# Sixteen of the prompt's expert rows moved from the merge into the latent q and k part of a diffusion trunk step

## The chip, the cores and the metric

The kernel runs on one core of a Trainium2 chip. The metric is the device time of one execution in microseconds (us). A core has TensorE (PE, matrix products), VectorE (DVE), ScalarE (ACT), GpSimd (POOL) and SyncE (SP), which each work through a program of their own in order and wait for one another on semaphores. SP issues the loads of the weights. POOL issues the gathers of expert rows, and each gather costs POOL an instruction before the DMA engines move anything.

## What is computed

The reference is a trunk of two layers over 128 prompt tokens and 512 latent tokens, all in float32. In each layer, and with the same weights for both kinds of tokens:

- an adaptive norm gives `h`; from it four branches are made: pooling over 2 to 16 neighbours, neighbourhood attention, a gated convolution over 31 tokens (`u = a * sigmoid(b)`, a depthwise convolution, a layer norm, SiLU), and differential attention; q and k are normed per head, and in the latent's differential branch they are rotated by position;
- the branches are merged with sigmoid gates and projected, `x = x + g1 * y`;
- a second norm, then the expert layer: each token takes 8 x 16 of 16384 experts and computes `sum(gate * gelu(u[e] . h) * v[e])`.

```python
s1, i1 = lax.top_k(s[:, :, 0], 16); s2, i2 = lax.top_k(s[:, :, 1], 16)
sc, ci = lax.top_k(s1[..., :, None] + s2[..., None, :], 16)      # 16 of 256 pairs
e = i1[ci // 16] * 128 + i2[ci % 16]; g = softmax(sc)
y = sum over 128 pairs of g * gelu(u_tab[e] . h) * v_tab[e]
```

## The kernel before

Tokens lie in tiles of 128. In the expert layer a tile has 128 pairs, and "row i" is pair i of all 128 tokens: one gather brings 128 lines of 8 KB (the expert's `u` and `v`, 1 MB in all) into a row buffer. The work on a row is a dot with `h` on DVE, the gelu and the gate factor on ACT, and the weighted sum.

**The order of the work in a layer.** The prompt tile is a layer's work ahead: its mixer, second norm and query scores are done before the latent tokens' layer begins (for layer 1 they are threaded into layer 0's latent expert rows). Then comes the latent part, which this case is about:

1. the front: the norm of the 512 latent tokens; eight projections for the gated convolution (`cb0 ca0 ... cb3 ca3`), four for pooling, eight units of v, and then the **q and k part**, 16 units of 128 tokens;
2. attention, 48 jobs: 16 differential ones first, then 32 of the neighbourhood kind;
3. the merge, 32 steps, each with a gate projection, half a branch projection, a sigmoid on ACT (L987) and a product on DVE (L1609);
4. the output projection for the first 256 tokens, 8 steps ("out"), their second norm, and 16 query steps ("query") with the latent's first routing from query step 8 on;
5. the expert rows of the four latent tiles, 512 rows, which begin when that first routing is done.

**What a prompt row is, and where it stands.** `prompt_dot` (L1374) multiplies and sums the `u` half with the prompt's `h`. `prompt_weights` (L826, L827) applies gelu and gate on ACT. `prompt_add` (L1381, L1384) adds the weighted `v` half to `yacc`. `prompt_rows` does dot i, then add i-1. `prompt_rows_at` deals the 128 rows out: 13 for every 4 merge steps (3, 3, 3, 4), one for each out step, two for each of the first 8 query steps. The gathers (L648) go through four buffers `prow`: gather i waits until add i-4 is done. They are issued by POOL from the moment at which attention has ended, after it has issued the load of the sub-keys.

**What stands in the q and k part.** PE projects unit n (8 products, recorded in 16 passes) into one of four PSUM banks, then transposes the normed unit n-2 (L1995). At unit 6 it adds the column sums for the convolution's layer norm, at unit 11 those of the squares. ACT squares the unit (L874), takes a root (L878) and copies the transposed unit out (`qk_out`). DVE takes the mean of unit n (L1482), norms unit n-1 (L1490 to L1513), and then does nine steps of `prompt_route`, the prompt's top-16 search (L1118 to L1181, 70 steps for each of two groups of heads). After unit 6, 11 and 12 it centres the convolution's result (L1519), takes its variance (L1525) and norms it (L1529, L1530). ACT's four squares of the convolution (L901) and its root come between its steps of the units.

**The gated blocks.** For block c, DVE waits for the projection `ca{c}` and multiplies it with ACT's sigmoid (L1460). The bank that it frees is what a later projection of PE goes into. Behind the four blocks stand 124 taps of the convolution (L1470, L1472), back to back on DVE.

**POOL's order in the front.** It clears two buffers, issues four loads, does the pooling windows (`pool_means`, L608 to L611) as their projections come, waits for ACT's two stores of v, issues 32 loads of the window copies of v (L621, into `vwin`), and then loads and masks the attention bias for heads 0 and 1 (L630, L635), which the first neighbourhood job needs. `prompt_gates` (ACT) and `prompt_soften` (DVE), the softmax of the prompt's gates, stand after attention.

Of the kernel before, what the change touches and what calls it, by code (L numbers as in the profile page):

```python
# [233 lines left out]
NP = 4  # L234

# [41 lines left out]
def backbone(nc, xT, cT, w, ada, small, rowg, lamrow, clay, poolw, subk, rope, edge, mask, bias, ckn, ckd,  # L277
             cvn, cvd, experts, y_prompt, y_sample, o_nk, o_nv, o_dk, o_dv):
    with ExitStack() as cx:
# [113 lines left out]
        yacc = at(arena, 22656, D)  # L393
# [19 lines left out]
        p_row = [sem(f"p_row{i}") for i in range(NP)]  # L413
        p_dot, p_w, p_acc = sem("p_dot"), sem("p_w"), sem("p_acc")
# [52 lines left out]
        def wait_unit(eng, key):  # L467

            if key in ENDS:
                eng.wait_ge(w_done[ENDS[key] % RING], ENDS[key] // RING + 1)  # L470
            else:
                eng.wait_ge(turn[key[0]], TURN[key] + 1)

# [40 lines left out]
        def _(gp):  # L514
# [77 lines left out]
            for l in range(DEPTH):  # L592
# [47 lines left out]
                for i in range(PAIRS):  # L640
                    n = l * PAIRS + i
                    if i % GP == 0:
                        gp.wait_ge(p_idx, 2 * l + i // GP + 1)
                    if i >= NP:
                        gp.wait_ge(p_acc, n - NP + 1)
                    if i == 3:
                        gp.wait_ge(y_diff, 4 * (l + 1))
                    gp.indirect_dma_start(prow[i % NP], None, experts,  # L648
                                          bass.IndirectOffsetOnAxis(ap=peidx[:, i:i + 1], axis=0)).then_inc(p_row[i % NP], 16)

# [24 lines left out]
        def _(act):  # L675
# [144 lines left out]
            def prompt_weights(l, which):  # L820

                for i in which:
                    if i % GP == 0:
                        act.wait_ge(p_gok, 2 * l + i // GP + 1)
                    act.wait_ge(p_dot, l * PAIRS + i + 1)
                    own.link(act.activation(pgel[:, i:i + 1], pdots[:, i:i + 1], ACT.Gelu))  # L826
                    act.activation(pwcol[:, i:i + 1], pgel[:, i:i + 1], ACT.Copy, scale=pgate[:, i:i + 1]).then_inc(p_w, 1)  # L827
# [10 lines left out]
            for l in range(DEPTH):  # L838
# [78 lines left out]

                for n in range(NQ + 2):
                    if n < NQ:
                        qk_square(n)  # L920
                    if 1 <= n <= NQ:
                        qk_rt(n - 1)
                    if n >= 2:
                        qk_out(n - 2)
                    if n == LNM_AT:
                        conv_squares()
                    if n == LNV_AT:
                        conv_root()
                    if n == LNV_AT + 3:
                        conv_silu()  # L930
# [41 lines left out]
                prompt_gates(l)  # L972
# [119 lines left out]
        def _(v):  # L1092
# [274 lines left out]
            def prompt_dot(l, i):  # L1367

                v.wait_ge(p_row[i % NP], (l * (PAIRS // NP) + i // NP + 1) * 16)
# [3 lines left out]
                e = prow[i % NP][:, 0:D]  # L1373
                v.tensor_tensor_reduce(e, e, htok(NL), 1.0, 0.0, ALU.mult, ALU.add, pdots[:, i:i + 1]).then_inc(p_dot, 1)  # L1374

            def prompt_add(l, i):

                v.wait_ge(p_w, l * PAIRS + i + 1)
                row = prow[i % NP][:, D:2 * D]
                if i == 0:  # L1380
                    v.tensor_scalar(yacc, row, pwcol[:, i:i + 1], None, ALU.mult).then_inc(p_acc, 1)  # L1381
                else:
                    v.wait_ge(p_acc, l * PAIRS + i)
                    v.scalar_tensor_tensor(yacc, row, pwcol[:, i:i + 1], yacc, ALU.mult, ALU.add).then_inc(p_acc, 1)  # L1384

            def prompt_rows(l, which):

                for i in which:
                    prompt_dot(l, i)
                    if i:  # L1390
                        prompt_add(l, i - 1)
# [10 lines left out]
            for l in range(DEPTH):  # L1402
# [143 lines left out]
                for _ in routing_steps:  # L1546
                    pass
# [33 lines left out]
                prompt_soften(l)  # L1581
# [739 lines left out]
```

## Time and profile before

| | |
|---|---|
| runs of the kernel | 5213.39 us median of 3 (5212.19 to 5225.22) |
| the profiled execution's own time | 5220.28 us |
| its span, first to last instruction | 5218.5 us |
| PE busy | 4457.4 us, 85% |
| DVE busy | 3365.3 us, 64% |
| ACT busy | 1875.6 us, 36% |
| POOL busy | 1779.1 us, 34% |
| granted PE clock, mean | 0.959 of full |

How to read it: everything that follows was read from that one execution. An engine's busy share is an average over stages with different limits, so the stages are read one by one. In a row of a timeline the first number is the start in us from the span's start and the second the length; in brackets stands the idle time before it and what ended it. In a row of a group stand the busy time and the mean length of one in ns, then the idle time before the group's instructions. A view by stretch tells the busy time of each engine in it, the granted clock of PE and what the DMA engines moved.

### The profile page before, as it was taken

What the parts mean: (1) busy time and instruction counts of PE and PEld (TensorE: products, weight loads), DVE (VectorE), ACT (ScalarE), POOL (GpSimd) and SP (SyncE); (2) the same over time, 40 slices, a digit from 0 to 9 for tenths busy, and PEclk for the clock granted to TensorE, in tenths of its full rate; (3) what the DMA queues carried; (4) which work ended last, traced back from release to release, by engine and by line L of the source; (5) the groups of instructions that cost most, each with busy time, mean ns of one, the idle gap of its engine ahead of it and who ended that gap; (6) DMA issues with size and microseconds to landing.
All of it is one profiled execution on the core that took longest, in us unless ns stands there. A gap on an engine that the chain in (4) does not pass through costs nothing.

```text
span 5218.5 us, 46810 instructions
## 1 busy us (share of the span) xinstructions
PE 4457.4 (85%) x14388; PEld 2301.6 (44%) x14388; DVE 3365.3 (64%) x7266; ACT 1875.6 (36%) x5016; POOL 1779.1 (34%) x1600
## 2 busy tenths in 40 slices
PE   7889888987799888888888998998879987777777
PEld 4674354334546333345544445633454632222222
DVE  4227856777787677675444486777777767676544
ACT  1210244433233433565533013534323343333333
POOL 3007202232243453443332460232324443434332
PEclk8799999998899999999999998999989999999999
DMA  7752227998799999999999131399979999999998
GB/s 287 253 181 73 89 91 263 348 343 338 291 420 419 412 420 420 413 398 418 405 420 400 57 97 33 116 347 340 354 275 420 419 412 421 421 421 420 418 421 359
DMA packets 277115, 1677.26 MB, mean 321 GB/s; under 512 B 31809, under 2 KB 31857, under 8 KB 112385
## 3 DMA queue, kind: packets, MB, share of 16 engines
q0 software_dynamic: 190896, 1365.43, 64.8%
q1 hardware_dynamic: 82944, 302.03, 16.0%
q10 hardware_dynamic: 3024, 6.82, 0.3%
q8 instruction: 115, 1.88, 0.1%
q14 instruction: 136, 1.11, 0.1%
HBM read 1667.33 MB, written 6.82 MB: 321 GB/s over the span
## 4 chain that ended last, share of the span: by engine, by line
DMA 38%; PE 35%; DVE 14%; ACT 7%; issue 5%; POOL 0%; SPq 0%; DVEq 0%; ACTq 0%; POOLq 0%
DMA arena<-experts,bsb 25%; PE ps L2194 13%; DMA arena<-experts,peidx 12%; PE ps L1781 8%; PE ps L1956 3%; DVE arena L1684 3%; PE ps L1889 2%; DMA wring<-w 2%; DVE arena L1384 2%; PE ps L2046 2%; PE ps L2068 2%; ACT L1047 1%; PE ps L1757 1%; ACT T L1051 1%; ACT L792 1%
## 5 line engine op out<-in xcount | busy, mean ns | idle before, releaser
L2194 PE MATMUL ps<-arena,T 128*128 128x512 f32 x4096 | 1965.3, 613 | 443.5 <-ACT T L1051 441.2
L1684 DVE CUSTOM_DVE_ANT_0 arena<-arena,h_sb 128x1024 f32<-128x1024 f32 x1024 | 1250.5, 1225 | 863.2 <-DMA arena<-experts,bsb 852.6
L665 POOL DMA_INDIRECT arena<-experts,bsb x1024 | 1094.6, 1069 | 1728.5 <-PE ps L2194 1586.4
L2194 PEld LDWEIGHTS ps<-arena,T 128*128 128x128 f32 x4096 | 725.2, 191 | 1566.5 <-ACT T L1051 943.9
L1047 ACT ACTIVATE bsb<-T 128x1 f32<-128x1 f32 x1024 | 205.9, 201 | 1307.5 <-DVE T L1684 1304.2
L1781 PE MATMUL ps<-h_sb,wring 128*128 128x256 f32 (+2 forms) x2304 | 532.6, 389 | 34.9 <-DVE h_sb L1424 13.7
L2105 PE MATMUL ps<-h_sb,wring 128*128 128x512 f32 x1024 | 479.8, 624 | 65.2 <-DVE arena L1609 58.4
L648 POOL DMA_INDIRECT arena<-experts,peidx x256 | 293.2, 1145 | 698.3 <-DVE arena L1384 646.0
L1781 PEld LDWEIGHTS ps<-h_sb,wring 128*128 128x128 f32 x2304 | 391.5, 201 | 188.5 <-issue 152.4
L1051 ACT ACTIVATE T<-ident,bsb 128x128 f32<-128x128 f32 x1024 | 410.9, 401 | 33.5
L1374 DVE CUSTOM_DVE_ANT_0 arena<-arena,h_sb 128x1024 f32<-128x1024 f32 x256 | 313.1, 1224 | 160.4 <-DMA arena<-experts,peidx 159.0
L2105 PEld LDWEIGHTS ps<-h_sb,wring 128*128 128x128 f32 x1024 | 201.9, 200 | 337.8 <-issue 254.5
L1956 PE MATMUL ps<-wring,h_sb 128*128 128x512 f32 x768 | 339.5, 600 | 0.0
L1384 DVE SCALAR_TENSOR_TENSOR arena<-arena,T 128x1024 f32<-128x1024 f32 x254 | 325.2, 1280 | 2.2 <-ACT T L827 2.2
L1048 ACT ACTIVATE bsb<-bsb,T 128x1 f32<-128x1 f32 x1024 | 301.5, 294 | 33.3
L826 ACT ACTIVATE T<-T 128x1 f32<-128x1 f32 x256 | 51.9, 203 | 565.8 <-DVE T L1374 565.8
L2110 PE MATMUL ps<-arena,wring 128*128 128x512 f32 x512 | 230.2, 592 | 0.0
L1956 PEld LDWEIGHTS ps<-wring,h_sb 128*128 128x128 f32 x768 | 146.4, 193 | 176.5 <-issue 176.5
L608 POOL COPY bsb<-arena 128x512 f32<-128x512 f32 x8 | 154.4, 19305 | 106.2 <-ACT arena L852 105.2
L1781 PE MATMUL ps<-arena,wring 128*128 128x256 f32 (+1 forms) x768 | 150.3, 352 | 23.5 <-DVEq L1615 22.6
L2046 PE MATMUL ps<-arena 64*128 64x128 f32 (+2 forms) x512 | 148.5, 424 | 18.8 <-ACT T L941 16.7
L1470 DVE SCALAR_TENSOR_TENSOR arena<-arena,sm 128x512 f32<-128x512 f32 x240 | 159.2, 743 | 0.0
(319 smaller groups left out, 4417.2 us busy)
## 6 DMA issues: line engine op xcount, KB each, us to landing
wring<-w SPq DMA_DIRECT2D x576, 512.0 KB
arena<-experts,bsb POOLq DMA_INDIRECT x1024
bsb<-bias POOLq DMA_DIRECT2D x16, 512.0 KB, 3.8
arena<-subk POOLq DMA_DIRECT2D x4, 1024.0 KB, 10.0
arena<-v_scratch POOLq DMA_DIRECT2D x64, 64.0 KB, 2.0
arena<-experts,peidx POOLq DMA_INDIRECT x256
x_sb<-xT POOLq DMA_DIRECT2D x1, 2048.0 KB, 14.2
v_scratch<-arena ACTq DMA_DIRECT2D x8, 256.0 KB, 2.0
```

Of the source, the lines that this page charges most:

```text
L648: gp.indirect_dma_start(prow[i % NP], None, experts, bass.IndirectOffsetOnAxis(ap=peidx[:, i:i + 1], axis=0)).then_inc(p_row[i % NP], 16)
L665: gp.indirect_dma_start(rows[:, n % NS, :], None, experts, bass.IndirectOffsetOnAxis(ap=eidx[:, t % 2, i:i + 1], axis=0)).then_inc(row_in[ ...
L1047: own.link(act.activation(gel[:, i:i + 1], dots[:, t % 2, i:i + 1], ACT.Gelu))
L1048: own.link(act.activation(wcol[:, i:i + 1], gel[:, i:i + 1], ACT.Copy, scale=gate[:, t % 2, i:i + 1]))
L1051: act.activation(diag[:, n % ND, :], ident[:], ACT.Copy, scale=wcol[:, i:i + 1]).then_inc(diag_ok, 1)
L1374: v.tensor_tensor_reduce(e, e, htok(NL), 1.0, 0.0, ALU.mult, ALU.add, pdots[:, i:i + 1]).then_inc(p_dot, 1)
L1384: v.scalar_tensor_tensor(yacc, row, pwcol[:, i:i + 1], yacc, ALU.mult, ALU.add).then_inc(p_acc, 1)
L1684: v.tensor_tensor_reduce(e, e, htok(t), 1.0, 0.0, ALU.mult, ALU.add, dots[:, t % 2, i:i + 1]).then_inc(dot, 1)
L1781: mm = pe.matmul(bank(key, cols), chunk_of(s, l, c)[:, k * P:(k + 1) * P], src(k), start=(k == 0), stop=(k == KD - 1))
L1956: mm = pe.matmul(bank(key), h_sb[:, t, k, :], chunk_of("L", l, c0 + q)[:, kk * 512:(kk + 1) * 512], start=(k == 0), stop=(k == KD - 1))
L2105: mm = pe.matmul(ps[:, s % 2, :], chunk_of("L", l, c)[:, k * P:(k + 1) * P], h_in(k), start=(k == 0), stop=(k == KD - 1))
L2194: mm = pe.matmul(ps[:, 6 + half, :], diag[:, n % ND, :], rows[:, n % NS, D + half * 512:D + (half + 1) * 512], start=(i == 0), stop=(i == ...
```

## The change

Rows 0 to 15 (`EARLY = 16`) are taken in the q and k part, one with each unit; 16 to 111 in the merge, three with each step; 112 to 119 in the out steps; 120 to 127 in the first 8 query steps, one each.

- **DVE**: `prompt_route` now runs ahead of the gated blocks, 36 of its steps before each, and not in the q and k part. `prompt_soften` stands before the q and k part. There each unit is followed by dot n-1 and add n-2 of the early rows.
- **ACT**: `prompt_gates` stands before the q and k part; after `qk_out(n-2)` comes the weight of row n-2.
- **POOL**: after the wait for the stores of v, and before the 32 window loads, it issues the 16 early gathers. They have two buffers of their own (`prow0`), which lie where `vwin` will be; gather i waits for add i-2, and the window loads wait for add 15.
- The early rows' dots, gelus and weights lie in `stp`, their sum in `yacc0`, which the add of row 16 takes up. Row 16 on goes through the four buffers as before.

```diff
+EARLY = 16
 def prompt_rows_at(stage, n):
     if stage == "merge":
-        return range(13 * n // 4, 13 * (n + 1) // 4)
+        return range(EARLY + 3 * n, EARLY + 3 * n + 3)
     if stage == "out":
-        return range(104 + n, 105 + n)
-    return range(112 + 2 * n, 114 + 2 * n) if n < 8 else ()
+        return range(112 + n, 113 + n)
+    return range(120 + n, 121 + n) if n < 8 else ()
...
+        prow0 = [at(arena, a, 2 * D) for a in (20096, 22144)]
+        yacc0, yacc = at(arena, 25728, D), at(arena, 22656, D)
...
                 for i in range(2):
                     gp.wait_ge(vb_out[i], 32 * (l + 1))
+                gp.wait_ge(p_idx, 2 * l + 1)
+                for i in range(EARLY):
+                    if i >= 2:
+                        gp.wait_ge(p_acc, l * PAIRS + i - 1)
+                    pause(gp)
+                    gp.indirect_dma_start(row_of(i), None, experts,
+                                          bass.IndirectOffsetOnAxis(ap=peidx[:, i:i + 1], axis=0)).then_inc(p_row0[i % 2], 16)
+                gp.wait_ge(p_acc, l * PAIRS + EARLY)
                 pause(gp)
                 vg = vscr.rearrange("(r c) n -> r c n", c=GRID_W)
...
-                for i in range(PAIRS):
-                    n = l * PAIRS + i
-                    if i % GP == 0:
-                        gp.wait_ge(p_idx, 2 * l + i // GP + 1)
-                    if i >= NP:
-                        gp.wait_ge(p_acc, n - NP + 1)
-                    if i == 3:
+                gp.wait_ge(p_idx, 2 * (l + 1))
+                for i in range(EARLY, PAIRS):
+                    if i >= EARLY + NP:
+                        gp.wait_ge(p_acc, l * PAIRS + i - NP + 1)
+                    if i == EARLY + 3:
                         gp.wait_ge(y_diff, 4 * (l + 1))
...
+                prompt_gates(l)
                 for n in range(NQ + 2):
...
                     if n >= 2:
                         qk_out(n - 2)
+                        prompt_weights(l, (n - 2,))
...
                 job_out(NJOBS - 1)
-                prompt_gates(l)
...
                 v.wait_ge(u_zero, l + 1)
+                routing_steps = prompt_route(l)
                 for c in range(4):
+                    for _ in range(36):
+                        next(routing_steps, None)
                     wait_unit(v, u(f"ca{c}"))
...
-                routing_steps = prompt_route(l)
+                assert next(routing_steps, None) is None
+                prompt_soften(l)
                 for n in range(NQ + 1):
...
                     if n >= 1:
                         qk_norm(n - 1)
-                        for _ in range(9):
-                            next(routing_steps, None)
+                        prompt_rows(l, (n - 1,))
...
-                for _ in routing_steps:
-                    pass
+                prompt_add(l, EARLY - 1)
...
                     job_probs(n)
-                prompt_soften(l)
```

## Rows read from the trace of the kernel before

**Rows 1.** Page, costliest groups: a row's dot (L1374), its add (L1384).
```profile
L1374 DVE CUSTOM_DVE_ANT_0 arena<-arena,h_sb 128x1024 f32<-128x1024 f32 x256 | 313.1, 1224 | 160.4 <-DMA arena<-experts,peidx 159.0
...
L1384 DVE SCALAR_TENSOR_TENSOR arena<-arena,T 128x1024 f32<-128x1024 f32 x254 | 325.2, 1280 | 2.2 <-ACT T L827 2.2
```

**Rows 2.** Busy time by stretch, layer 0: merge, query, q and k part.
```profile
core 0: us, PE busy (x) PEld busy (x) DVE busy (x) ACT busy (x) POOL busy (x), PEclk, DMA share, GB/s
873.90:1256.00 382.10, 341.49 (x765) 150.55 (x764) 283.86 (x366) 153.25 (x300) 119.41 (x103) 0.94 0.92 343
...
1298.00:1358.00 60.00, 41.43 (x185) 34.71 (x184) 41.43 (x58) 12.07 (x43) 15.38 (x13) 0.90 0.85 315
...
499.00:652.00 153.00, 134.58 (x343) 61.68 (x341) 122.03 (x352) 32.49 (x69) 51.02 (x71) 0.93 0.27 84
```

**Rows 3.** Groups by line, VectorE, 364.7 to 416.9 us: gated blocks.
```profile
L1460 DVE TENSOR_TENSOR arena<-ps,T 128x512 f32<-128x512 f32 x4 | 2.8, 692 | 49.4 <-PE ps L1781 49.4
```

**Rows 4.** Groups by line, VectorE, 2890 to 3200 us: routing, branch norm.
```profile
L1174 DVE TENSOR_TENSOR arena<-arena 128x1024 f32<-128x1024 f32 x4 | 4.9, 1226 | 0.1
...
L1529 DVE RECIPROCAL T<-T 128x512 f32<-128x512 f32 x1 | 3.3, 3333 | 0.0
...
L1530 DVE TENSOR_TENSOR arena<-arena,T 128x2048 f32<-128x2048 f32 x1 | 2.3, 2293 | 0.0
...
L1165 DVE TENSOR_SCALAR arena<-arena 128x64 uint32<-128x64 uint32 x2 | 0.4, 186 | 0.0
```

**Rows 5.** Timeline (start us, length us) of VectorE behind the taps, layer 0.
```profile
506.03 0.69 DVE L1482 TENSOR_REDUCE st<-T 128x8 f32<-128x512 f32 x1 [7.63 <-ACT T L874]
...
512.90 0.69 DVE L1482 TENSOR_REDUCE st<-T 128x8 f32<-128x512 f32 x1 [5.93 <-ACT T L874]
```

**Rows 6.** Timeline of GpSimd, layer 0: first pooling copy, first window load.
```profile
423.73 75.14 POOL L608 COPY bsb<-arena 128x512 f32<-128x512 f32 x1 [52.68 <-ACT arena L852]
...
530.19 15.72 POOL L621 DMA_DIRECT2D arena<-v_scratch  x32 [0.58 <-POOL arena L611]
```

**Rows 7.** Timeline, 1390 to 1400 us: first expert gather and first dot on it.
```profile
1392.68 0.94 POOL L665 DMA_INDIRECT arena<-experts,bsb  x1 [44.12 <-DVE bsb L1181]
...
1398.29 1.23 DVE L1684 CUSTOM_DVE_ANT_0 arena<-arena,h_sb 128x1024 f32<-128x1024 f32 x1 [4.30 <-DMA arena<-experts,bsb]
```

**Rows 8.** Timeline, one unit of the q and k part, layer 0.
```profile
530.53 0.68 DVE L1482 TENSOR_REDUCE st<-T 128x8 f32<-128x512 f32 x1
...
535.98 7.03 PE L1956 MATMUL ps<-wring,h_sb 128*128 128x512 f32 x16
```

**Rows 9.** Line L648, all prompt gathers: ns min/median/max.
```profile
L648 POOL DMA_INDIRECT arena<-experts,peidx x256: 932/937/1970, 852.3 to 3842.5; - x128
```

**Rows 10.** Busy time by stretch after TensorE stood still 10.9 us.
```profile
1402.00:1405.00 3.00, 3.00 (x4) 1.42 (x5) 1.93 (x5) 0.90 (x3) 1.49 (x1) 0.51 1.00 418
```

**Rows 11.** Timeline, first attention scores of layer 0.
```profile
652.62 1.36 PE L2046 MATMUL ps<-arena 64*128 64x512 f32 x8 [1.04 <-issue]
```

**Rows 12.** Timeline, merge of layer 0: products of steps 0, 10, 11, 12, 31.
```profile
873.89 0.68 DVE L1609 TENSOR_TENSOR arena<-ps,arena 128x512 f32<-128x512 f32 x1
...
990.34 0.69 DVE L1609 TENSOR_TENSOR arena<-ps,arena 128x512 f32<-128x512 f32 x1 [1.40 <-ACT arena L987]
...
1001.02 0.69 DVE L1609 TENSOR_TENSOR arena<-ps,arena 128x512 f32<-128x512 f32 x1 [1.40 <-ACT arena L987]
...
1015.98 0.69 DVE L1609 TENSOR_TENSOR arena<-ps,arena 128x512 f32<-128x512 f32 x1 [1.40 <-ACT arena L987]
...
1245.04 0.69 DVE L1609 TENSOR_TENSOR arena<-ps,arena 128x512 f32<-128x512 f32 x1 [1.40 <-ACT arena L987]
```

**Rows 13.** Timeline, query stage, layer 0: TensorE's step, first latent routing.
```profile
1303.94 3.62 PE L1781 MATMUL ps<-h_sb,wring 128*128 128x256 f32 x16
1307.39 0.61 PE L2135 MATMUL ps<-arena,T 128*128 128x128 f32 x4
...
1359.14 1.63 DVE L1118 MAX8 bsb<-arena 128x8 f32<-128x128 f32 x8
```

More of the change, by code:

```diff
@@ L413, in backbone @@
         p_row = [sem(f"p_row{i}") for i in range(NP)]
+        p_row0 = [sem(f"p_row0{i}") for i in range(2)]
         p_dot, p_w, p_acc = sem("p_dot"), sem("p_w"), sem("p_acc")
@@ L472, in wait_unit, with row_of, weight_of @@
                 eng.wait_ge(turn[key[0]], TURN[key] + 1)
+        def row_of(i):
+            return prow0[i % 2] if i < EARLY else prow[i % NP]
+        def weight_of(i):
+            return stp[:, i:i + 1] if i < EARLY else pwcol[:, i:i + 1]
         def chunk_of(s, l, c):
@@ L639, in _ @@
                 gp.dma_start(sk, subk[l]).then_inc(subk_in, 16)
[L640 to L646 removed]
+                gp.wait_ge(p_idx, 2 * (l + 1))
[3 more added lines that the diff above has]
+                    if i == EARLY + 3:
                         gp.wait_ge(y_diff, 4 * (l + 1))
[L648 removed]
+                    gp.indirect_dma_start(row_of(i), None, experts,
                                           bass.IndirectOffsetOnAxis(ap=peidx[:, i:i + 1], axis=0)).then_inc(p_row[i % NP], 16)
@@ L825, in prompt_weights @@
                     act.wait_ge(p_dot, l * PAIRS + i + 1)
-                    own.link(act.activation(pgel[:, i:i + 1], pdots[:, i:i + 1], ACT.Gelu))
-                    act.activation(pwcol[:, i:i + 1], pgel[:, i:i + 1], ACT.Copy, scale=pgate[:, i:i + 1]).then_inc(p_w, 1)
+                    d = stp[:, i:i + 1] if i < EARLY else pdots[:, i:i + 1]
+                    g = stp[:, i:i + 1] if i < EARLY else pgel[:, i:i + 1]
+                    own.link(act.activation(g, d, ACT.Gelu))
+                    act.activation(weight_of(i), g, ACT.Copy, scale=pgate[:, i:i + 1]).then_inc(p_w, 1)
             mixer = prompt_mixer(0)
@@ L1367, in prompt_dot @@
             def prompt_dot(l, i):
-                v.wait_ge(p_row[i % NP], (l * (PAIRS // NP) + i // NP + 1) * 16)
+                if i < EARLY:
+                    v.wait_ge(p_row0[i % 2], (l * (EARLY // 2) + i // 2 + 1) * 16)
+                else:
+                    v.wait_ge(p_row[i % NP], (l * ((PAIRS - EARLY) // NP) + (i - EARLY) // NP + 1) * 16)
                 if i == 0:
@@ L1372, in prompt_dot @@
                         wait_freed(v, ("P", l, name))
-                e = prow[i % NP][:, 0:D]
-                v.tensor_tensor_reduce(e, e, htok(NL), 1.0, 0.0, ALU.mult, ALU.add, pdots[:, i:i + 1]).then_inc(p_dot, 1)
+                e = row_of(i)[:, 0:D]
+                d = stp[:, i:i + 1] if i < EARLY else pdots[:, i:i + 1]
+                v.tensor_tensor_reduce(e, e, htok(NL), 1.0, 0.0, ALU.mult, ALU.add, d).then_inc(p_dot, 1)
             def prompt_add(l, i):
                 v.wait_ge(p_w, l * PAIRS + i + 1)
-                row = prow[i % NP][:, D:2 * D]
+                row = row_of(i)[:, D:2 * D]
                 if i == 0:
-                    v.tensor_scalar(yacc, row, pwcol[:, i:i + 1], None, ALU.mult).then_inc(p_acc, 1)
+                    v.tensor_scalar(yacc0, row, weight_of(i), None, ALU.mult).then_inc(p_acc, 1)
                 else:
                     v.wait_ge(p_acc, l * PAIRS + i)
-                    v.scalar_tensor_tensor(yacc, row, pwcol[:, i:i + 1], yacc, ALU.mult, ALU.add).then_inc(p_acc, 1)
+                    v.scalar_tensor_tensor(yacc0 if i < EARLY else yacc, row, weight_of(i), yacc0 if i <= EARLY else yacc, ALU.mult, ALU.add).then_inc(p_acc, 1)
             def prompt_rows(l, which):
@@ L1389, in prompt_rows @@
                     prompt_dot(l, i)
-                    if i:
+                    if i not in (0, EARLY):
                         prompt_add(l, i - 1)
```

1 line of the change is left out of this document (removed).

## The prediction

> **What bounds the kernel now.** I first read the stretches of the stages that the change touches [rows 2]. In the merge PE is busy 341 of 382 us and DVE 284, while the DMA engines are busy 0.92 of the time: three resources near their limits, and a dot that often waits for its gather (160.4 us before 256 dots [rows 1]). In eight query steps the clock runs 60 us for 41 us of PE work and 41 of DVE work. So each prompt row there costs time. In the q and k part PE has 135 us of work in 153 and the DMA share is 0.27: there is room for transfers but hardly any for a longer chain. Then I looked for idle time that could pay: DVE waits 49.4 us for the four gated projections [rows 3], and once more behind the taps, 7.63 and 5.93 us [rows 5]. The latent expert stage is not touched; it only starts earlier or later.
>
> All times below are of layer 0 of the profiled execution; layer 1 is taken to be its copy.
>
> **1. Routing goes ahead of the gated blocks.** Its 28 groups add up to 62.0 us busy, from 4.9 down to 0.4 [rows 4], but short instructions overlap: eight MAX8 take 1.63 us [rows 13]. I take 57 us of elapsed time. It meets 49.4 us of idle time [rows 3]; the first quarter holds the short searches and leaves 1.7 us of its wait over. The taps start 57 - 49.4 + 1.7 = 9.5 us later. Two things hide it. A delayed product holds a PSUM bank back, but its next user comes one to two projections (6.9 us each) later, so PE loses nothing. And behind the taps DVE waits 13.6 us for units that PE has not finished [rows 5]; those 9.5 us and the 1.3 us of the softmax fit in. Cost: nothing; without that cover, 9.5 us a layer. The softmax leaves the path behind attention: 0.9 us a layer gained, ACT's exponentials with it.
>
> **2. The first early row is late.** GpSimd's first pooling copy starts at 423.73 and is held 75.1 us, until the taps are over; the first window load comes at 530.19, 31.3 us behind the copy's end at 498.87 [rows 6]. The early gathers stand in that place in POOL's program, behind the pooling work. With the taps 9.5 us later, and 1 us less contention because DVE will stand still, the first gather is issued at 498.9 + 9.5 + 31.3 - 1 = 538.7. From the issue of a first gather to its dot the expert stage takes 1398.29 - 1392.68 = 5.6 us [rows 7]. Dot 0 starts at 544.3. DVE has normed unit 0 at about 519 and has nothing else in its order: it waits some 25 us with dot 0, and behind it stand the mean of unit 2 and the norm of unit 1, for which PE's transposes, and so its units 4 and later, wait.
>
> **3. The pace of the early rows.** With two buffers gather n is issued after add n-2, at the end of a unit's work, and dot n comes at the end of the next. So one unit takes at least the gather's latency plus a dot and an add, 1.22 + 1.28 = 2.5 us [rows 1]. No row shows a gather by itself. The nearest is the 5.6 us of rows 7, with a second gather 1.2 us behind it that shares the engines: I take 5.3, so 7.8 us a unit. Below it cannot fall under PE's 7.5 us (7.03 for a unit's passes and the transposes [rows 8]). Above stands the latency in the merge: there a row takes 3.7 us with three gathers in flight, (3 x 3.7) - 2.5 = 8.6 us, so 11.1 a unit; the q and k part moves a quarter as much beside it, so I stay at the low end. Under the latency DVE's norm work is hidden: from a mean to PE's next unit 5.4 us [rows 8], half of it for the neighbourhood units.
>
> From dot 0 to dot 15 that is 15 x 7.8 = 117 us. Row 1 is already there: -1.8. Behind unit 6 the centring (about as long as the 2.3 us product of L1530) and ACT's squares of it are no longer filled by routing: +5.7. Variance and root: +1. The reciprocal and product, 3.3 + 2.3 us [rows 4], less 2.7 that the latency hides: +2.9. PE stands still for some 23 us and comes back slow: after 10.9 us of standing its granted clock was 0.51, the 1.2 GHz level, for 3 us of work [rows 10]; with the units that follow, +2. Dot 15 starts at 544.3 + 126.8 = 671.1. Its dot, gelu and weight (1.9 us) stand in ACT's order ahead of the four copies of the pooling products (2.9 us), for which the first attention scores wait: 676.2 against 652.62 [rows 11]. **The front costs 23.6 us a layer.** Late next are the window loads and the first bias, about 32 us of POOL; 16 differential jobs (80 us) run before they are needed, so they cost nothing.
>
> **4. GpSimd's issue of a gather.** The median is 0.937 us, the longest 1.97 [rows 9]: beside DVE's dots and adds some are held for up to 1 us, and a long row of taps held a copy for 75 us [rows 6]. I take 0.94, since an early gather is issued when DVE turns to the mean, which reads one operand.
> By the Trainium skill (SBUF — State Buffer, section "SBUF: two separate sides") GpSimd and VectorE lock a shared pair of ports against each other, and a GpSimd-issued DMA cannot write its descriptors while VectorE holds it; the copy of rows 6 agrees, the median of rows 9 does not for gathers. By that rule the sum would have the longest issue each time, which is rival C.
>
> **5. The merge gets 8 rows fewer.** From step 0 to step 31 it takes 1245.04 - 873.89 = 371.1 us, seven of the steps with four rows [rows 12]. One with four takes 15.0 us (1001.02 to 1015.98), the one before it with three 10.7; over the layer I read 14.7 against 11.3. So an extra row costs 3.4 us, more than its 2.5 us on DVE, because sigmoid and product of the next step wait behind it. PE's own 12 products of a step take 10.3 us, so three rows do not yet lie below PE. Gain: 8 x 3.4 = 27.4 us. The out steps keep a row each: nothing.
>
> **6. The query steps get 8 rows fewer.** From 1298.0 [rows 2] to the first latent routing at 1359.14 [rows 13] the 8 steps take 61.1 us. With one row a step PE is next: 3.45 us and a scoring, 3.9 us a step [rows 13]; the transfers (1 MB of a row and 0.5 MB of weights) come to 4.1. The first score can be taken at 1304.2, seven steps of 4.15 end at 1333.3, the last add 1.5 later. Gain: 24.3 us.
>
> **Sum.** A layer: 23.6 - 0.9 - 27.4 - 24.3 = -29.0 us; both: -58. The profiled execution stands at 5220.3, 7 us above the median of the runs, so the median goes to 5213.4 - 58 = **5155 us**.
>
> **Rivals.**
> - **A, slower: early gathers are as slow as the merge's.** Their latency is 8.6, a unit takes 11.1 us, 15 x 3.3 = 50 us more a layer: 5213 + 2 x 21 = 5255. It decides from a unit of 9.8 us on, a latency of 7.3. Against it: DMA share 0.27. For it: the weight ring and the bias can bunch. 0.08.
> - **B: no wait at the first row.** Were POOL's pooling work done between the routing instructions before the taps, dot 0 would come 25 us earlier: 5106. Against it: its inputs are only there at 423.73 and later, one by one, and the taps start at 426. 0.06.
> - **C: each early issue is held by DVE.** 1.97 instead of 0.94 us, 16 times, up to 15 us a layer: 5185. 0.10.
> - **D: a row taken out saves only DVE's time.** If transfers or PE are next at once in merge and query, the gain is 16 x 2.5 = 40 us a layer instead of 51.7: 5178. For it: PE 0.89 and DMA 0.92 busy in the merge. 0.14.
> - **E: PE's wait moves to the gated blocks** because a bank is freed late there, up to 9.5 us a layer: 5174. 0.04.
>
> **The numbers.** The forecast has 0.58. Range: 5115 to 5190; it takes in C, D and E, the lower bound of the pace (15 x 0.3 us a layer, 5146) and a first wait shortened by half (5130), and leaves out A and the lowest of B. A measurement of this kernel can tell about 0.3% (16 us) from no change, so the borders are 5198 and 5229. Faster: forecast, B, E and nearly all of C and D, 0.86. C and D together would be 5208, and a unit near 9.5 us lies there too: within, 0.07. Slower: most of A, 0.07.
>
> **What would show it.** In the changed profile: the last L1460 about 10 us later than now with PE's products unbroken; the first early gather near 539 and its dot near 544, after an idle time of about 25 us; one dot every 7.8 us from there; attention's first scores near 676; merge steps of about 11.3 us, all alike; the first latent routing 24 us closer to the start of the query steps. The forecast is wrong if dots in the q and k part come further apart than 9.8 us, if merge steps stay near 12 us, or if the first dot does not wait.

## The result and the profile after

The changed kernel takes 5163.98 us (median of 4 runs, 5152.61 to 5172.88) against 5219.31 us (5212.19 to 5227.35) of the kernel before on the same chip: ratio 0.9893, 95% interval 0.9874 to 0.9913, **faster by 1.1%**, about 56 us. The forecast was 5155 us, that is 58 less. The profiled execution took 5164.73 us, its span 5162.9 against 5218.5. The mean granted clock is 0.964 against 0.959.

First the page of the changed kernel: its span and busy times, and the groups that answer to [rows 1] and to the gathers of [rows 9]. L1396 is a row's dot, L1406 its add, L1495 a tap, L630 an early gather.

```profile
span 5162.9 us, 46892 instructions
...
PE 4427.5 (86%) x14388; PEld 2284.0 (44%) x14388; DVE 3387.4 (66%) x7266; ACT 1951.4 (38%) x5074; POOL 1663.2 (32%) x1600
...
L1396 DVE CUSTOM_DVE_ANT_0 arena<-arena,h_sb 128x1024 f32<-128x1024 f32 x256 | 312.6, 1222 | 186.8 <-DMA arena<-experts,peidx 185.5
...
L1406 DVE SCALAR_TENSOR_TENSOR arena<-arena,T 128x1024 f32<-128x1024 f32 x224 | 286.7, 1280 | 0.1
...
L1495 DVE SCALAR_TENSOR_TENSOR arena<-arena,sm 128x512 f32<-128x512 f32 x240 | 184.9, 846 | 0.0
L630 POOL DMA_INDIRECT arena<-experts,peidx x32 | 65.6, 2048 | 342.2 <-DVE arena L1406 228.3
```

DVE does the same work and is busy 22 us longer than before (3387.4 against 3365.3). Look at L1495: a tap now takes 846 ns, and 240 of them make 25 us more than in the page of before, where a tap is L1470:

```profile
L1470 DVE SCALAR_TENSOR_TENSOR arena<-arena,sm 128x512 f32<-128x512 f32 x240 | 159.2, 743 | 0.0
```

ACT is busy 76 us longer (1951.4 against 1875.6), though it computes the same: between the roots of the units it now has to do a gelu for each early row, and it loads a function table each time it turns from one to the other, 58 loads of 1.28 us more than before. The forecast had no term for them. An early gather takes 2048 ns on the mean, because of one odd instruction among 16, as the timeline below shows.

The stages of layer 0, by stretch: merge, first eight query steps, q and k part. They answer to [rows 2].

```profile
core 0: us, PE busy (x) PEld busy (x) DVE busy (x) ACT busy (x) POOL busy (x), PEclk, DMA share, GB/s
903.40:1256.70 353.30, 326.25 (x753) 142.99 (x752) 267.05 (x345) 148.61 (x285) 108.78 (x95) 0.98 0.93 348
1288.30:1326.00 37.70, 33.30 (x161) 29.50 (x162) 29.71 (x50) 8.76 (x27) 6.36 (x6) 0.90 0.77 298
513.00:671.00 158.00, 121.19 (x302) 55.93 (x304) 105.35 (x190) 75.67 (x126) 19.47 (x20) 0.87 0.44 160
```

The merge and its step to the first out product is 31 us shorter; the q and k part has become the stretch with idle engines (PE 121 of 158 us). The ledger by stages is this, in us, each length read between two instructions of the timeline. "Front" runs from the sum of the first latent norm to the first maximum of the attention scores.

| stage, layer 0 / layer 1 | before | after | difference | forecast |
|---|---|---|---|---|
| front | 302.7 / 302.7 | 327.1 / 324.7 | +24.3 / +22.0 | +23.6 |
| attention to merge | 219.9 / 178.7 | 231.8 / 176.5 | +11.9 / -2.2 | -0.9 |
| merge to first out product | 384.2 / 387.4 | 353.3 / 358.1 | -30.9 / -29.3 | -27.4 |
| second norm to first expert gather | 103.1 / 99.6 | 76.0 / 76.4 | -27.0 / -23.1 | -24.3 |

The differences add up to -54.5; the spans differ by 55.6. The attention stage of layer 0 is not steady: over the nine profiles that this case has (before, after and seven experiments) it took 219.9 to 257.2 us with the same instructions, while that of layer 1 took 175 to 182. Its length goes with the granted clock of PE in it: 219.9 us at 0.95 (before), 221 to 223 at 0.93, 225 to 232 at 0.90 to 0.92 (231.8 at 0.91 in the changed kernel), and 257.2 at 0.79. For the same products PE was busy 190.0 us before and 199.5 in the changed kernel, 9.5 us more, where the stage is 11.9 us longer. So this row is mostly one of the clock; what brings the clock down there, and whether the change has a part in it, no run shows.

Now the timelines of layer 0. First GpSimd, which answers to [rows 6]:

```profile
417.00 0.61 POOL L617 COPY bsb<-arena 128x512 f32<-128x512 f32 x1 [52.61 <-ACT arena L869]
...
423.86 1.08 POOL L617 COPY bsb<-arena 128x512 f32<-128x512 f32 x1 [1.00 <-ACT arena L869]
...
453.10 1.59 POOL L620 TENSOR_TENSOR arena<-bsb 128x512 f32<-128x512 f32 x1
498.24 18.23 POOL L630 DMA_INDIRECT arena<-experts,peidx  x1 [43.56 <-issue]
516.78 0.96 POOL L630 DMA_INDIRECT arena<-experts,peidx  x1 [0.30 <-issue]
531.03 0.94 POOL L630 DMA_INDIRECT arena<-experts,peidx  x1 [13.30 <-DVE arena L1403]
...
561.46 0.94 POOL L630 DMA_INDIRECT arena<-experts,peidx  x1 [7.56 <-DVE arena L1406]
569.94 0.94 POOL L630 DMA_INDIRECT arena<-experts,peidx  x1 [7.54 <-DVE arena L1406]
```

and VectorE, from the last gate product (L1485) over the first taps to the dots (L1396), an add (L1406) and the first attention maximum (L1583):

```profile
419.07 0.68 DVE L1485 TENSOR_TENSOR arena<-ps,T 128x512 f32<-128x512 f32 x1
419.91 3.24 DVE L1497 TENSOR_SCALAR arena<-arena,sm 128x512 f32<-128x512 f32 x4
...
516.96 0.67 DVE L1507 TENSOR_REDUCE st<-T 128x8 f32<-128x512 f32 x1
...
522.49 1.22 DVE L1396 CUSTOM_DVE_ANT_0 arena<-arena,h_sb 128x1024 f32<-128x1024 f32 x1
...
540.92 1.23 DVE L1396 CUSTOM_DVE_ANT_0 arena<-arena,h_sb 128x1024 f32<-128x1024 f32 x1 [2.03 <-DMA arena<-experts,peidx]
...
558.26 1.22 DVE L1396 CUSTOM_DVE_ANT_0 arena<-arena,h_sb 128x1024 f32<-128x1024 f32 x1 [1.33 <-DMA arena<-experts,peidx]
559.41 0.08 DVE L1396 DVE_READ_ACCUMULATOR2_ANT stp<- 128x1 f32 x1
559.41 1.28 DVE L1406 SCALAR_TENSOR_TENSOR arena<-arena,stp 128x1024 f32<-128x1024 f32 x1
...
664.69 1.22 DVE L1396 CUSTOM_DVE_ANT_0 arena<-arena,h_sb 128x1024 f32<-128x1024 f32 x1 [6.05 <-DMA arena<-experts,peidx]
...
671.62 0.82 DVE L1583 TENSOR_REDUCE st<-ps 128x1 f32<-128x640 f32 x1 [3.10 <-PE ps L2069]
```

Two things are not as forecast. The first copy of the pooling work takes 0.61 us and not 75, since it now starts 2.9 us ahead of the taps (417.00 and 419.91), where before it started 6.8 us behind them (423.73 [rows 6] and 416.98, shown below), and POOL is through with all of that work at 454.7. The taps take from 419.91 to 515.5, 14 us longer than before. So the first early gather is issued while they still run; it is held until they end (18.23 us, to 516.5), and dot 0 at 522.49 has no wait ahead of it. The forecast had it wait 25 us. The row of before that the 6.8 us are taken from is the first four taps of layer 0:

```profile
416.98 1.92 DVE L1472 TENSOR_SCALAR arena<-arena,sm 128x512 f32<-128x512 f32 x4
```

### The profile page after: what moved, and what is told of

The parts are those of the page before. It is cut to its first block, busy times and chain, and to the rows that moved or that the text cites. A ratio compares the mean times of both kernels' runs of the same rounds, so it can differ in the third digit from the quotient of the medians.

```text
span 5162.9 us, 46892 instructions
## 1 busy us (share of the span) xinstructions
PE 4427.5 (86%) x14388; PEld 2284.0 (44%) x14388; DVE 3387.4 (66%) x7266; ACT 1951.4 (38%) x5074; POOL 1663.2 (32%) x1600
## 4 chain that ended last, share of the span: by engine, by line
DMA 42%; PE 29%; DVE 17%; ACT 6%; issue 6%; POOL 0%; SPq 0%; DVEq 0%; ACTq 0%; POOLq 0%
DMA arena<-experts,bsb 26%; DMA arena<-experts,peidx 13%; PE ps L2217 13%; PE ps L1804 5%; DVE arena L1495 4%; DVE arena L1707 3%; DVE arena L1406 2%; PE ps L1912 2%; DMA wring<-w 2%; PE ps L2069 2%; PE ps L2091 2%; PE ps L1780 1%; ACT T L1069 1%; ACT L1065 1%; ACT bsb L1066 1%
## 5 line engine op out<-in xcount | busy, mean ns | idle before, releaser
L1804 PE MATMUL ps<-h_sb,wring 128*128 128x256 f32 (+2 forms) x2304 | 517.4, 381 | 35.5 <-DVE h_sb L1446 13.7
L2128 PE MATMUL ps<-h_sb,wring 128*128 128x512 f32 x1024 | 457.4, 600 | 33.7 <-DVE arena L1632 31.5
L1804 PEld LDWEIGHTS ps<-h_sb,wring 128*128 128x128 f32 x2304 | 379.9, 196 | 184.6 <-issue 152.6
L663 POOL DMA_INDIRECT arena<-experts,peidx x224 | 251.5, 1123 | 617.3 <-DVE arena L1406 581.5
L1396 DVE CUSTOM_DVE_ANT_0 arena<-arena,h_sb 128x1024 f32<-128x1024 f32 x256 | 312.6, 1222 | 186.8 <-DMA arena<-experts,peidx 185.5
L2128 PEld LDWEIGHTS ps<-h_sb,wring 128*128 128x128 f32 x1024 | 192.3, 191 | 294.6 <-issue 229.4
L1406 DVE SCALAR_TENSOR_TENSOR arena<-arena,T 128x1024 f32<-128x1024 f32 x224 | 286.7, 1280 | 0.1
L1495 DVE SCALAR_TENSOR_TENSOR arena<-arena,sm 128x512 f32<-128x512 f32 x240 | 184.9, 846 | 0.0
L630 POOL DMA_INDIRECT arena<-experts,peidx x32 | 65.6, 2048 | 342.2 <-DVE arena L1406 228.3
```

What stands on the lines that cost most here:

```text
L1406: v.scalar_tensor_tensor(yacc0 if i < EARLY else yacc, row, weight_of(i), yacc0 if i <= EARLY else yacc, ALU.mult, ALU.add).then_inc(p_acc, 1)
L1495: op = v.scalar_tensor_tensor(acc[:, c, :], U[:, c, 1 + k:1 + k + LAT], S(col), acc[:, c, :], ALU.mult, ALU.add)
L1804: mm = pe.matmul(bank(key, cols), chunk_of(s, l, c)[:, k * P:(k + 1) * P], src(k), start=(k == 0), stop=(k == KD - 1))
L2128: mm = pe.matmul(ps[:, s % 2, :], chunk_of("L", l, c)[:, k * P:(k + 1) * P], h_in(k), start=(k == 0), stop=(k == KD - 1))
```

## The experiments

The theory after this reading: **whether POOL's first copy comes ahead of the taps or behind their start decides who pays.** Behind it, POOL is held until the taps end and DVE pays nothing (before). Ahead of it, both work side by side and each of DVE's taps is longer (after). The delay of the taps by the routing is what swapped the two. Rivals: that the taps are longer for another reason (the routing, the other buffers), or that the pace of the early rows comes from DVE or PE and not from the gather. Times of layer 0 are measured from the norm's sum, as the front starts some us earlier or later from one kernel to the next. Each ratio is to the kernel before as it was measured again beside the experiments: 5214.34 us for the routing alone, the later pooling, the pause and the three buffers, 5219.85 us for the other three. Where two numbers are given for a front, they are layer 0 and layer 1.

**The routing alone.** From the kernel before, with only the order of DVE's and ACT's work changed; all rows where they were.

```diff
+                routing_steps = prompt_route(l)
                 for c in range(4):
+                    for _ in range(36):
+                        next(routing_steps, None)
...
-                routing_steps = prompt_route(l)
+                prompt_soften(l)
                 for n in range(NQ + 1):
...
-                        for _ in range(9):
-                            next(routing_steps, None)
```

> Of the change only the routing and the softmax of the prompt's gates are moved ahead; all 128 rows stay in merge, out and query steps as before. Theory 1 (the pooling work of GpSimd gets in between the taps because its first copy comes before they start): taps end some 96 us behind the last gate product instead of 82, the q and k part then runs at PE's 7.5 us a unit, and from the norm's sum to the first attention scores a layer takes 303 to 309 us against 302.8 before; total 5205 to 5230 us, no change that can be told. Theory 2 (the taps are slow in the changed kernel because of the early gathers): taps stay at 82 us, the front becomes 8 to 11 us a layer shorter, total near 5200.

Measured: 5207.56 us (10 runs), ratio 0.9993 (0.9976 to 1.001): no difference that can be told. From the last gate product to the end of the taps it takes 96.4 us against 82.3, so the longer taps come with the routing's new place and not with the early rows. But the front is 297.1 us, 5.7 **shorter** than before, where 303 to 309 was expected. From the first mean to the last the q and k part takes 111.3 us against 129.0: the routing's 57 us of DVE time are out of it, and the units that PE has meanwhile finished are there at once. That more than pays for the first mean being 17 us late.

**The old order of pooling and taps given back.** From the changed kernel; the pooling work waits until the first 12 of the 124 taps have been issued.

```diff
                         own.tick(op)
+                    if k == 2:
+                        v.sem_inc(tap_mid, 1)
...
+                gp.wait_ge(tap_mid, l + 1)
```

> The changed kernel, but GpSimd waits with its pooling work until the first 12 taps are done. Theory 1 (a GpSimd operation that reads SBUF and comes while taps run back to back is held until they end; one that comes before them goes on alternating): the first pooling copy is held some 70 us, the taps are back at 82 us, dot 0 waits some 25 us and stands some 193 us behind the norm's sum (178 in the changed kernel), as the prediction had it; the front costs 10 to 15 us a layer more than in the changed kernel, total 5180 to 5195. Theory 2 (what comes first does not matter): the copy takes about 1 us, the taps 95 us, and the total stays at 5160 to 5170.

Measured: 5202.9 us (10 runs), ratio 0.9974 (0.9955 to 0.9993), and in the timelines of GpSimd and VectorE of this kernel (L619 is the copy, L632 the early gather, L1398 the dot):

```profile
429.81 77.10 POOL L619 COPY bsb<-arena 128x512 f32<-128x512 f32 x1 [59.94 <-DVEq L1502]
...
537.84 1.07 POOL L632 DMA_INDIRECT arena<-experts,peidx  x1 [0.90 <-POOL arena L622]
539.22 0.96 POOL L632 DMA_INDIRECT arena<-experts,peidx  x1 [0.30 <-issue]
```
```profile
543.54 1.23 DVE L1398 CUSTOM_DVE_ANT_0 arena<-arena,h_sb 128x1024 f32<-128x1024 f32 x1 [25.23 <-DMA arena<-experts,peidx]
```

The copy is held 77 us, the taps are back at 82.3 us, and the path of the forecast appears piece by piece: the gather 187.8 us behind the norm's sum (forecast 187.5), a wait of 25.23 us (some 25), dot 0 193.5 us behind the sum (193.1). The front is 9.6 and 14.7 us longer than in the changed kernel, 336.7 and 339.4. So the 14 us on the taps buy more than they cost here. The total lies 8 us above the range that was expected. In the profile the attention stage of layer 0 took 257.2 us, 25 more than in the changed kernel, at a granted clock of 0.79 against 0.91; but the profiled execution (5222.48 us) was 20 us above the median of the ten, so this stage does not explain the median. The mean clocks of the ten runs lie lower too, 0.952 to 0.963 against 0.961 to 0.966. So the total carries more than the order of pooling and taps; the front, the copy and the dot are what this run shows.

**The swap brought about in the kernel before.** Its taps wait until the first copy is issued; nothing else is changed.

```diff
+                    if g == 0:
+                        gp.sem_inc(first_copy, 1)
...
+                v.wait_ge(first_copy, l + 1)
                 for k in range(CONV_W):
```

> The kernel before with one wait more: VectorE starts the taps only when GpSimd's first pooling copy is done. Theory 1 (whoever has the ports goes on; only a copy that meets running taps is held): the copy takes about 0.6 us instead of 75, the taps start some 8 us later and take 96 us instead of 82, so the first mean comes 11 to 15 us later than before; the q and k part is bound by VectorE there and gives nothing back: total 5235 to 5245. Theory 2 (the routing ahead of the gated blocks is what opens the way for GpSimd): the copy is held again, or the taps stay at 82 us, and the total is 5214 to 5222.

Measured: 5236.88 us (10 runs), ratio 1.0031 (1.0012 to 1.005), slower. Timelines of GpSimd (the copy, then the 32 window loads) and VectorE, then the group of the taps (L1474) of layer 0:

```profile
421.62 0.61 POOL L609 COPY bsb<-arena 128x512 f32<-128x512 f32 x1 [52.81 <-ACT arena L855]
...
502.46 15.73 POOL L624 DMA_DIRECT2D arena<-v_scratch  x32 [43.33 <-DMA v_scratch<-arena]
```
```profile
422.31 3.57 DVE L1476 TENSOR_SCALAR arena<-arena,sm 128x512 f32<-128x512 f32 x4 [7.59 <-POOLq L611]
```
```profile
L1474 DVE SCALAR_TENSOR_TENSOR arena<-arena,sm 128x512 f32<-128x512 f32 x120 | 93.5, 859 | 0.0
```

Without routing ahead, without early rows and with the buffers of before, the copy takes 0.61 us instead of 75.14 [rows 6] and a tap 859 ns instead of 743. With the three kernels above (the changed one, the routing alone, the later pooling) this settles the theory: the order of the two starts sets both lengths. By itself it costs 7.3 and 6.3 us of front a layer, since here no early row gains from POOL's being free. The window loads are worth a look: they are issued from 502.46 to 518.19, all while the taps run (until 519.3), after GpSimd has stood idle for 43 us, and each takes 0.5 us. They are not held, unlike the first early gather, which stands in this place of POOL's program in the changed kernel.

**The pace of a unit.** First the empty instruction ahead of each early gather is taken out (`pause(gp)`), from the changed kernel.

```diff
-                    pause(gp)
                     gp.indirect_dma_start(row_of(i), None, experts,
```

> The changed kernel without the empty instruction ahead of each early gather. Theory 1 (the pace of the early rows is add, issue delay, latency, dot; the empty instruction is 0.5 us of the 0.77 between add and issue): a unit goes from 8.5 to 8.0 us, 6 to 8 us a layer, total 5148 to 5156. Theory 2 (the pace is set by TensorE or ScalarE): no change, 5160 to 5168.

Measured: 5156.37 us (4 runs), ratio 0.9886 (0.986 to 0.9913), which cannot be told from the changed kernel's. In its timelines the add (L1405) and the gather that waits for it (L629):

```profile
559.83 1.28 DVE L1405 SCALAR_TENSOR_TENSOR arena<-arena,stp 128x1024 f32<-128x1024 f32 x1
...
561.38 0.94 POOL L629 DMA_INDIRECT arena<-experts,peidx  x1 [7.46 <-DVE arena L1405]
```

The gather starts 0.27 us behind the add's end. In the changed kernel it is 0.77 us (559.41 + 1.28 = 560.69, and the gather at 561.46). In layer 0 a steady unit takes 8.1 to 8.4 us instead of 8.5 to 8.8, and the front is 5.4 and 4.2 us shorter.

Then a third buffer for the early rows, in the changed kernel, pause left in. It lies in the buffers of the pooling work, which is over by then; gather i waits for add i-3.

```diff
-        prow0 = [at(arena, a, 2 * D) for a in (20096, 22144)]
+        prow0 = [at(arena, a, 2 * D) for a in (20096, 22144)] + [at(bsb, 0, 2 * D)]
+        NE = len(prow0)
...
-                    if i >= 2:
-                        gp.wait_ge(p_acc, l * PAIRS + i - 1)
+                    if i >= NE:
+                        gp.wait_ge(p_acc, l * PAIRS + i - NE + 1)
```

> The changed kernel with a third buffer for the early rows, in the space of the pooling's work buffers. Theory 1 (the gather's latency with two buffers sets the pace): the waits of the early dots on their gathers vanish, a unit goes from 8.5 to 7.5 or 7.8 us, 10 to 15 us a layer, total 5134 to 5148. Theory 2 (TensorE, ScalarE or VectorE sets it): the waits move to the units' squares and the total stays above 5155.

Measured: **5122.34 us** (4 runs, 5105.29 to 5138.46), ratio 0.9823 (0.979 to 0.9856), 92 us less than the kernel before beside it: better than both kernels, and 12 us better than the range expected. DVE's waits in the q and k part, first in the changed kernel (517 to 668 us), then in this one (521 to 650 us); columns are us in total, times, longest:

```profile
DVE arena L1396 <- DMA arena<-experts,peidx: 37.4, 12, 6.1
DVE st L1507 <- ACT T L891: 7.2, 4, 3.1
```
```profile
DVE st L1508 <- ACT T L892: 15.4, 5, 4.6
DVE st L1516 <- ACT st L896: 3.4, 6, 0.6
```

The waits for gathers are gone; what is left waits for ACT's squares, that is for PE. And in the timeline PE's units follow one another (L1980):

```profile
544.57 7.03 PE L1980 MATMUL ps<-wring,h_sb 128*128 128x512 f32 x16
...
551.44 0.60 PE L2019 MATMUL ps<-ident,T 128*128 128x128 f32 x4
...
551.87 7.03 PE L1980 MATMUL ps<-wring,h_sb 128*128 128x512 f32 x16
```

One unit takes 7.3 us here, PE's own time. The front is 303.1 and 302.8 us: what it was before the change, with 16 rows in it. So most of what the early rows cost the changed kernel was the gather's latency under two buffers; the next run tells how much.

**The early rows left out.** From the changed kernel; rows 0 to 15 of each layer are neither gathered nor computed for the prompt, so their share is missing from its result, and the rest stands as it was. This prices 16 rows from both sides.

```diff
-                for i in range(EARLY):
...
-                    gp.indirect_dma_start(row_of(i), None, experts,
...
-                        prompt_rows(l, (n - 1,))
```

> The changed kernel with the 16 early rows left out of the computation (no gather, dot, weight or add for them); everything else stands where the change put it. Against the run with routing alone it shows what 16 rows fewer in merge and query steps bring. Theory 1 (a row there costs 3.1 to 3.7 us): merge and query together 50 to 58 us a layer shorter than with all rows in them, total 5090 to 5105. Theory 2 (rival D, a row costs only VectorE's 2.5 us): 40 us a layer, total near 5130. The front should take 297 us from the norm's sum to the first scores, as with routing alone; the rest up to the changed kernel's 325 to 327 us is then the price of the early rows.

Measured: 5107.54 us (4 runs), ratio 0.9788 (0.976 to 0.9816). The merge and the query part by stretch, of this kernel, then of the one with the routing alone, which does all rows in merge and query:

```profile
868.40:1224.30 355.90, 328.89 (x756) 144.33 (x755) 266.24 (x345) 148.62 (x285) 107.24 (x95) 0.97 0.92 345
1256.70:1333.40 76.70, 69.02 (x344) 60.76 (x344) 61.51 (x170) 15.38 (x39) 6.38 (x6) 0.92 0.58 205
```
```profile
871.90:1256.00 384.10, 340.75 (x771) 151.01 (x770) 285.88 (x369) 153.79 (x302) 121.92 (x103) 0.95 0.91 344
1286.80:1383.40 96.60, 75.53 (x344) 64.22 (x344) 79.75 (x193) 19.13 (x55) 14.63 (x14) 0.87 0.69 250
```

Eight rows save 384.1 - 355.9 = 28.2 us in the merge, 3.5 a row, and 19.9 in the query part, 2.5 a row; in layer 1 it is 22.7 and 19.6. That is 45 us a layer, 2.8 a row; the medians of the two kernels, 100 us apart, give 3.1, and 3.3 if each is set against the kernel before beside it (7 and 112 us less). Profiles differ by some us in these stages, so it is better to take them together: the three kernels with all 128 rows in merge, out and query take 384.7 us for the merge and 98.6 for the query part on the mean of both layers, the six with 112 of them take 356.9 and 76.9. That is 27.8 + 21.7 = 49.5 us a layer, 3.1 a row, at the lower edge of the 50 to 58 us expected. And compared with the changed kernel, whose front is 327.1 and 324.7 us against 297.1 here, its 16 early rows cost 29.9 and 27.6 us of front; with three buffers 5.9 and 5.7.

**The tail of the front.** With three buffers and no pause, ACT takes the copies of the pooling products ahead of the last early weight, as the forecast had named that order as a delay for the first scores.

```diff
-                        prompt_weights(l, (n - 2,))
+                        if n < NQ + 1:
+                            prompt_weights(l, (n - 2,))
...
+                prompt_weights(l, (EARLY - 1,))
```

> Three buffers for the early rows, no empty instruction ahead of their gathers, and ScalarE copies the four pooling products out before it makes the weight of the last early row. Theory 1: the last two early rows no longer stand ahead of attention; the front falls from 303 us with three buffers to 299 to 301, total 5114 to 5124. Theory 2 (with three buffers nothing of the front waits for ScalarE any more): front 303, total as with three buffers alone, 5118 to 5128.

Measured: 5124.88 us (4 runs), ratio 0.9824 (0.9796 to 0.9853), the front 302.8 and 303.1. Order and pause together bring nothing that can be told once there are three buffers; they were not tried one by one there.

## Why the prediction was right, and where it was not

The total is right within 9 us and the front within 2, but the second is partly luck: two steps that were wrong cancel. By its own signs the forecast even counts as wrong in the front: "if the first dot does not wait" was one of them, and it did not wait; "further apart than 9.8 us" was another, and five of the 15 distances between the early dots of layer 0 are longer (12.5, 12.9, 10.3, 11.8 and 10.1), though not the steady ones. Some of its sums are off by little: 57 - 49.4 + 1.7 is 9.3 and not 9.5, 671.1 + 1.9 + 2.9 is 675.9 and not 676.2, 8 x 3.4 is 27.2 and not 27.4, and seven merge steps of 14.7 with 24 of 11.3 make 374 us and not 371.1. None of this moves the total by more than 2 us. In the ledger the total is a sum of misses as well: over both layers merge and query bring 110 us where 103 were forecast, and the attention stages take 10 us more where 2 less were forecast.

- **Step 1, routing ahead.** The shift is right: behind the norm's sum the last gate product comes 9.6 us later (9.5 forecast), and DVE has no idle time left ahead of the products. "Cost: nothing" is right for the shift and missed what it sets off. The forecast had both numbers of the changed kernel, 423.73 for the copy and 426 for the taps, and used them only to say that the pooling work cannot be over before the taps. It did not see that by these very numbers the copy, so far behind the taps' start, would now be ahead of it. The taps grew by 14.2 us (layer 0). The first mean behind them came 9.6 + 14.2 + 1.4 (the softmax) - 7.6 (the wait of [rows 5], now gone) = 17.6 us later: 172.4 us behind the norm's sum against 154.8. The forecast also missed a gain: with the routing out of the units, the q and k part catches up, and the front by itself ends 5.7 us earlier.
- **Step 2, the first early row late.** This step failed: there was no wait at dot 0, which came 177.9 us behind the norm's sum against 193.1 forecast. Its chain was right for a kernel in which the copy is held, as the run with the pooling work held back shows to within 1 us, but that is not the kernel that the change makes. Rival B (no wait at the first row) had 0.06 and was argued away by "its inputs are only there at 423.73 and later", with the taps starting at 426. Its condition came true, but not its 5106: it priced the 25 us and not what the taps would pay.
- **Step 3, the pace.** The mechanism is right: with two buffers a unit is a latency plus a dot and an add. It was mis-sized at 7.8 us; dot to dot is 8.5 to 8.9 in the steady units. The 5.3 us of latency hold (561.46 to 566.73); left out was the time from the add's end to the gather's issue, 0.77 us, of which the empty instruction makes 0.5. The latency being the limit is shown by the third buffer: 7.3 us a unit, which is PE. From dot 0 to dot 15 it took 142.2 us against 126.8 forecast, 0.7 us a unit, some 10 us, of it by this. The rest are single longer steps. In the one from dot 1 to dot 2 (12.5 us) the gather has only a part: it was issued at 531.03 and met its dot 9.9 us later, yet the dot waited just 2.03 us for it. Ahead of that PE had stood still for 10.25 us until 522.62, came back at a granted clock of 0.50 (the 1.2 GHz level) and took 9.13 us for a unit's passes instead of 7.03, so that the mean of unit 2 waited 3.07 us. At dots 14 and 15 the gathers took 8.6 and 6.8 us. With dot 0 15 us early, the two errors leave a front of +24.3 and +22.0 against +23.6.
- **Step 4, the issue.** In the steady units 0.94 us, as taken, so rival C (1.97 us each) falls. The first one is the exception: 18.23 us, behind taps. By the Trainium skill (SBUF — State Buffer, section "SBUF: two separate sides") whichever of the two engines starts first has the shared ports for the whole instruction, and the other blocks, if VectorE's instruction has two inputs in SBUF and GpSimd's reads SBUF. The trace agrees with a lock, but not with one instruction as its length: a copy that met running taps was held for over 100 of them (75.14 us), a gather for the last 20 or so (18.23 us).
- **Steps 5 and 6, merge and query.** Right in mechanism and size. Over all profiles the merge gives 27.8 us a layer (27.4 forecast) and the query part 21.7 (24.3); the 27.0 us that the table above shows for the query part of layer 0 is flattered by the profile of before, whose 103.1 us is the longest of its kind. A row in the merge costs 3.5 us, more than its 2.5 on DVE, as forecast; one in the query steps 2.7, hardly more and less than the 3.0 forecast. Rival D (2.5 us for every row, 40 us a layer) falls: 49.5 by the stages, 50 to 53 by the medians of the two kernels that differ in the early rows alone.
- **Rivals A and E.** A (from a unit of 9.8 us on) was nearer than its 0.08 says: steady units take 8.5 to 8.9 us, but all 15 steps on the mean 142.2 / 15 = 9.5. A's mechanism, gathers slowed by bunched transfers, shows only here and there. In most units of the changed kernel a gather reached its dot in 5.3 to 5.7 us, with a DMA share of 0.5 to 0.8 between the two. Where the share was 0.81 to 0.88, three gathers took 8.4, 9.6 and 6.6 us, and the third gather of layer 0 (9.9 us) had four weight loads of 512 KB each beside it and a share of 0.87 from 533 to 539 us; but the last two of layer 0 took 8.6 and 6.8 us at 0.54 and 0.45. That bunching is the cause is not shown. E did not come: PE's products in the gated blocks are unbroken.

## What to carry to other kernels

When a change moves one engine's work by a few microseconds, list the instructions of other engines that start within that distance of it, and ask for each pair what happens if their order turns round: here a shift of 9.6 us turned 6.8 us behind into 2.9 us ahead, and that decided 14 us of taps and 15 us of the first row. Where gathers take turns in buffers, add up release, issue, latency and use as one loop and ask over how many units it spreads (one with two buffers here, two with three); if that is above the unit's own time, a buffer is worth more than any reordering. When work is moved into an idle engine's time, price it at its new place too: 16 rows cost 28 to 30 us a layer there with two buffers and 6 with three.

## What the runs showed of the hardware that was not expected

A GpSimd instruction that starts while DVE runs its taps back to back (float32, two operands in SBUF) can wait for the end of the whole run: copies of 75.14 and 77.10 us, a gather's issue of 18.23 us. Not every one does: in the run in which the taps wait for the copy, and in the one with the routing alone, the 32 window loads were issued during the taps at 0.5 us each (15.73 and 15.77 us in all), behind 43 us in which GpSimd was idle. The copy and the gather have something to read in SBUF (`arena`, and the row numbers in `peidx`), the window loads read only `v_scratch` in DRAM; that this makes the difference was not tried. But where GpSimd's work was already under way when the taps began, its next instructions also started among running taps and were not held (a copy at 423.86 behind a gap of 1.0 us, and all that follows until 454.7): the two go on side by side, a tap takes 846 to 859 ns instead of 743, and GpSimd's additions 1.35 us instead of 1.09. In the changed kernel that cost DVE 14 us, and the pooling work was over 110.1 us behind the norm's sum instead of 178.4.

What lets GpSimd keep its turn is open, and whether a short gap in the taps would let a held instruction in was not tried. The forecast's reading, that running taps always hold GpSimd, is the part of these rows that does not carry over.
